# Moving VectorE's addition of a finished projection group behind the weight subtraction of its turn

## The reference

```python
h = rms_norm(x, norm1_g) * (1 + sc1) + sh1          # sc, sh, g: six rows of silu(c) @ w_mod + b_mod
z = h @ w_in                                        # FoX q,k,v,forget | NSA q,k,v... | conv a,g
mixed = concat(fox_attention, nsa_attention, conformer_conv(a, g))
x = x + g1 * (mixed @ w_out)
h = rms_norm(x, norm2_g) * (1 + sc2) + sh2
x = x + g2 * (relu(h @ w_mlp1)**2 @ w_mlp2)
return rms_norm(x, final_g)
```

## Time and profile before

| | us |
|---|---|
| median of 3 runs | 1174.67 (1172.66 to 1175.06) |
| the profiled execution, its own time | 1174.19 |
| its span in the profile | 1172.2 |
| TensorE (PE) busy in the span | 1134.7 |
| VectorE (DVE) busy | 983.7 |
| ScalarE (ACT) busy | 641.5 |
| mean share of the granted TensorE clock | 0.989 |

### The profile page before, as it was taken

The page is one execution under the profiler, slowest core; times in us unless marked ns, Lnnn a source line. Parts: engine busy times, 40 slices in busy tenths (PEclk is TensorE's granted clock), DMA queues, the critical chain, the costliest instruction groups (busy, mean ns, idle before and its releaser), DMA issues.

```text
span 1172.2 us, 17842 instructions
## 1 busy us (share of the span) xinstructions
PE 1134.7 (97%) x7087; PEld 1005.2 (86%) x7087; DVE 983.7 (84%) x1182; ACT 641.5 (55%) x936; POOL 23.6 (2%) x40
## 2 busy tenths in 40 slices
PE   4999999999999999999999999999999999999996
PEld 4899989999887778999788888888888888888885
DVE  5998989988997988997887788987778987878774
ACT  6655458877775546544454445554455544445452
POOL 1000000100000000010000000000000000000000
PEclk6999999999999999999999999999999999999999
DMA  9999998878966897985657675657674667666451
GB/s 372 420 420 420 421 409 310 255 205 281 358 227 249 301 304 292 401 351 183 210 186 266 240 282 180 215 187 277 238 270 176 218 202 263 251 231 262 152 180 72
DMA packets 48322, 314.65 MB, mean 268 GB/s; under 512 B 6572, under 2 KB 8440, under 8 KB 11768
## 3 DMA queue, kind: packets, MB, share of 16 engines
q1 hardware_dynamic: 44592, 305.72, 70.1%
q0 software_dynamic: 1760, 5.26, 2.4%
q10 hardware_dynamic: 1896, 2.64, 0.8%
HBM read 305.20 MB, written 4.21 MB: 264 GB/s over the span
## 4 chain that ended last, share of the span: by engine, by line
PE 76%; DVE 11%; DMA 5%; ACT 4%; issue 3%; SPq 0%; ACTq 0%; DVEq 0%
PE quad L1285 15%; PE quad L1299 10%; PE quad L1300 10%; PE quad L1301 10%; PE quad L1287 8%; PE quad L1275 5%; PE quad L1276 5%; PE quad L1277 5%; DMA first_raw<-in_w_mod 3%; DVE w_lo L1850 3%; PE quad L1346 2%; PE quad L1345 2%; PE quad L1347 2%; DVE mod_raw L1857 2%; DMA mod_raw<-in_w_mod 2%
## 5 line engine op out<-in xcount | busy, mean ns | idle before, releaser
L893 ACT ACTIVATE w_hi<-raw 128x1024 fp32r<-128x1024 f32 (+1 forms) x342 | 355.4, 1044 | 304.9 <-PE quad L1301 115.9
L1850 DVE TENSOR_TENSOR w_lo<-raw,w_hi 128x1024 fp32r<-128x1024 f32 (+1 forms) x342 | 408.3, 1204 | 112.4 <-ACT w_hi L893 110.4
L1285 PE MATMUL quad<-act,w_hi 128*128 128x512 f32 x768 | 266.4, 390 | 0.0
L1275 PE MATMUL quad<-act,w_hi 128*128 128x256 f32 x760 | 215.2, 283 | 6.0 <-DVE w_lo L1850 3.9
L1287 PE MATMUL quad<-act,w_lo 128*128 128x256 f32 x768 | 216.6, 282 | 0.0
L1276 PE MATMUL quad<-act,w_hi 128*128 128x256 f32 x760 | 213.1, 280 | 0.0
L1277 PE MATMUL quad<-act,w_lo 128*128 128x256 f32 x760 | 213.1, 280 | 0.0
L1285 PEld LDWEIGHTS quad<-act,w_hi 128*128 128x128 f32 x768 | 144.2, 188 | 30.2
L1275 PEld LDWEIGHTS quad<-act,w_hi 128*128 128x128 f32 x760 | 144.1, 190 | 8.7 <-issue 4.6
L1299 PE MATMUL quad<-w_hi,u_hi 128*128 128x512 f32 x376 | 148.8, 396 | 0.6 <-DVE u_lo L2307 0.6
L1301 PE MATMUL quad<-w_hi,u_lo 128*128 128x512 f32 x376 | 148.7, 396 | 0.0
(11 more groups left out here) (371 smaller groups left out, 1715.6 us busy)
## 6 DMA issues: line engine op xcount, KB each, us to landing
raw<-in_w_main SPq DMA_DIRECT2D x184, 1024.0 KB, 5.0
mod_raw<-in_w_mod SPq DMA_DIRECT2D x67, 1024.0 KB, 7.2
first_raw<-in_w_mod SPq DMA_DIRECT2D x14, 1024.0 KB, 15.3
late_raw<-in_w_mod SPq DMA_DIRECT2D x10, 1024.0 KB, 7.9
acc<-in_w_mod SPq DMA_DIRECT2D x4, 1024.0 KB, 12.5
conv_b<-conv_q POOLq DMA_DIRECT2D x8, 512.0 KB, 5.2
x_a<-in_x SPq DMA_DIRECT2D x2, 1024.0 KB, 7.2
x_scratch<-x SPq DMA_DIRECT2D x1, 2048.0 KB, 11.7
```

The costliest lines, as they stand in the source:

```text
L893: A(dst[:, 0:2 * width], block_half(raw, j, width), ACT.Copy).then_inc(hi_done, 1)
L1275: mm(out, hi, act_hi[:, k, :], start=begin and m % 2 == 0, stop=False, skip_group_check=True)
L1285: mm(out, w_hi[j % 4][:, cols], act_both[:, k, :, :].rearrange("p h t -> p (h t)"), start=begin, stop=False, skip_group_check=True)
L1850: TTn(lo[:, 0:2 * width], block_half(raw, j, width), hi[:, 0:2 * width].bitcast(f32), ALU.subtract)\
```

## The change

VectorE's loop over turns gets the additions behind `weight_lo_in(half)` of the same turn in place of ahead of it (and behind `add_tap(-1)`, which no turn with an addition has). No other engine's program changes.

```diff
@@ -2148,13 +2148,13 @@
                         bias_scores(scored + 1)
                     if summed is not None and summed % 4 == 2:
                         outputs(summed // 4)
-                for u in ADDED:
-                    if turn == UNIT_END[u] + 3:
-                        add_result(u)
                 if turn == TAP_HALF:
                     add_tap(-1)
                 if half is not None:
                     weight_lo_in(half)
+                for u in ADDED:
+                    if turn == UNIT_END[u] + 3:
+                        add_result(u)
                 if 0 < turn - TAP_HALF - 1 <= CONV_W:
                     add_tap(turn - TAP_HALF - 1)
                 if turn - 1 in H_AT:
```

## The result

The changed kernel takes 1175.57 us (median of 20 runs, 1174.29 to 1178.74), the kernel before 1174.05 us (20 runs on the same chips, 1172.66 to 1175.55). The ratio is 1.0015, with a 95% interval from 1.0009 to 1.0022: slower by 1.5 us, which is clear of noise but within 0.2%. The forecast was +1.75 us, to 1176.4 from a median of before of 1174.67.

What follows compares the result with a forecast made beforehand. TensorE (97% busy) sets the time, near 200 us through VectorE's order. FV +1.13, FE +1.20, FA -1.13 and half 62's wait of 0.55 gave +1.75 us: 1176.4 against the median; range 1173.5 to 1178.2, widened by 0.1 and 0.3.

Steps and rivals of the forecast that it cites:

- The replay: VectorE, ScalarE and TensorE followed turn by turn in the new order: +1.2 to +2.3 us, likeliest +1.75; chance 0.62.
- Turn 51's lag: Turn 51: VectorE falls back 1.07 us as the subtraction awaits its cast; hidden up to turn 55.
- FV: Addition of turn 55: behind the subtraction it moves conv_in from 179.91 to 181.04, +1.13 us.
- FE: Addition of turn 57, in two pieces of 0.60 us: behind the subtraction it adds +1.20 us.
- FA: Addition of turn 61, ahead of the subtraction TensorE awaits: moving it behind counts -1.13 us.
- rival B: Lag made up before turn 61 through overlooked gaps, TensorE's gap falls to 0.29: -1.13 us, 1173.5; chance 0.13.
- Rival D: First scores (turn 75) don't shed VectorE's lag, one addition joins the chain: +3.5 us, 1178.2; chance 0.10.
- The second wait: TensorE at half 62, wanted at 205.42 and ready at 205.86: waits another 0.55 us.
- kept to the end, and no more: Behind 212 us VectorE and ScalarE catch up with TensorE, so the lost 1.75 us stays unchanged to the end.
- rival C: Later stages' waits not tied to TensorE (a DMA landing) give the loss back: 0, 1174.7; chance 0.11.
- rival E: TensorE's clock falls in the gap of 2.6 us: 1.75 + 2.5 = +4.3 us, 1179.0; chance 0.04.
- The gap is nearest to the first row, and I take no loss: TensorE's gap near 200 us likened to the profiled 1.42 us gap with clock 1.00 behind it: no clock loss.

Runs made afterwards that it cites:

- the late six: Only the additions of turns 65, 69, 75, 81, 87 and 91 put behind the subtraction, against the kernel before: 1174.04 us, ratio 1.0000.

## Why the prediction was right

**The replay held to 0.05 us at each step.** Half 51 at 164.80 (worked out 164.80), half 55 at 176.52 (176.51), conv_in at 181.06 (181.04), the cast of half 57 at 184.30 (184.29), the row product at 187.71 (187.70), half 61 at 201.25 (201.24), TensorE resumed at 202.62 (202.60), half 62 at 206.02 (205.97). The lag was 2.33 (2.32), the loss at the first scores 1.73 (1.75). That is the mechanism of the forecast, and it held.

**Its parts were each shown alone.** Turn 51's lag is hidden by the wait for half 55's cast only if turn 55 is swapped too; alone it costs 0.75. Net of the start of each execution, FV made VectorE late by 1.14 and FE by 1.21; FA gave 0.61 (1.13 at half 61 less what half 62 takes back), and the late six nothing. With the 0.75 of turns 51 and 53 hidden, the rest adds up: 1.14 + 1.21 - 0.61 = 1.74, and the whole lost 1.73 at the first scores.

**The tie of the cast to conv_in**, on which rival B hung, is shown by the tap moved behind the cast: the lag went. Rival D fell too: at the first scores VectorE waits 1.40 us for TensorE, more than the 1.16 before, and their +1.73 is TensorE's own 1.70 at half 62.

**What was off.** First, TensorE's gap was forecast as 2.6 us and was 2.26. The forecast took the end of a matmul (199.99) less 2.80 as the moment when TensorE wants half 60, 197.19. But a matmul starts 0.12 us behind the one before it while its row lasts 0.28, and before started half 60 at 197.04. So the half that was ready at 197.18 was not "just in time": TensorE started it at 197.32, 0.28 late, and the first matmul behind a wait costs 0.08 more (the next start comes 0.19 behind it in place of 0.12). So TensorE entered the gap 0.37 us later. The end of the gap was right, and so the time was not touched. The second wait, forecast as 0.55 from start to start, is 0.34 in its row, which counts from the modelled end of the last matmul.

Second, "kept to the end, and no more" failed. Near 411 us VectorE waits for a load; the read behind it came at 412.60 us in one and at 411.45 in another of two profiles with the same first scores. Of 1.73 us the first profile gave back 0.37 there and the third 1.51. This is rival C's mechanism, which had a chance of 0.11, at a fifth of its size in the one and nearly whole in the other.

Third, rival E had a chance of 0.04 and a price of 2.5 us. It is no rival but a part of the answer: in one profile of three the clock fell behind the changed kernel's gap, and the first scores came 0.95 us later for it. The step that failed is "The gap is nearest to the first row, and I take no loss": a single row at a gap of 1.42 couldn't speak for one of 2.3. The Trainium skill (TensorE: Matmul & The Clock Gate, "Part 1: The HAM clock gate") says that an idle array is throttled. In this case's traces the array lost its clock behind such a gap in five profiles of eight and kept it in three.

In the 20 runs, 6 lie from 1176.98 to 1178.74 and 14 from 1174.29 to 1175.90. The mean granted clock of the six is 0.987 in three, 0.988, 0.989 and 0.992 in the others, that of the fourteen 0.988 to 0.993. So the three slowest (1177.43, 1178.62 and 1178.74) have the three lowest clocks, which fits with a fall, and the one at 1176.98 with 0.992 doesn't fit. The rows of the six are not kept, so this is argued, not shown.

**How far the number is luck.** The order makes +1.73 at the first scores, and that was shown. The measured +1.5 of the medians has two more terms, one down (0.37 to 1.51 at the DMA wait of two profiles) and one up (0.95 where the clock fell). The forecast had both at nothing. Together they come to -0.2 by the medians. That they nearly cancel is luck, and how large each is on average stays open.

## What to carry to other kernels

Work that fills a wait is free only where it stands. Ahead of an operation that waits for another engine, a ready addition costs nothing; moved behind it, both the wait and the addition are on the path. So the order within a turn is to be read per turn: behind, where the awaited operand has long been there and the next engine hungers (turn 61); ahead, where it hasn't (51 to 57). And where an engine waits for a late operand (ScalarE for conv_in), look for something that others want and that could go first: against before, all swaps together cost 1.5 us, and with that one cast moved the same swaps cost nothing that was resolved (ratio 1.0003).

## What the runs showed of the hardware that was not expected

The granted TensorE clock fell to half behind gaps of 2.16 to 3.38 us in five profiles of eight; in two of these five another profile of the same program, with the same gap to 0.01 us, kept its clock. It didn't fall behind the two gaps of 1.42 and 1.43 at that place, but behind a wait of 1.5 us near 360 us it fell in two profiles of fourteen. A fall at 200 us cost 0.95 to 2.42 us at the first scores, 0.4 to 0.8 of the gap ahead of it.

The same DMA load of the same program, issued at 406.26 and 406.12 us, was waited for until 412.60 in one execution and was there by 411.45 in another, and that moved the end by 1.2 us. A load issued 0.81 us earlier landed no earlier for the engine that waited for it, so that a gain of 0.8 us vanished for ninety microseconds.
